# Where TensorE's rounded operands begin in SBUF: two blocks on one core

## What is computed

```python
def reference(x, ...):
    x = first_block(x, ...)      # one layer: four kinds of attention, gates, w_out, conv FFN (D_FF = 2816)
    return second_block(x, ...)  # two layers: FFN, four mixers, w_out, FFN, a gated embedding

def swiglu(x, w_gate, w_up, w_down):
    return (jax.nn.silu(x @ w_gate) * (x @ w_up)) @ w_down
```

## Time and profile before

| | |
|---|---|
| Median of 3 runs | 3416.65 us (3411.78 to 3417.28) |
| The profiled execution | 3416.89 us |
| Its span, first to last instruction | 3415.6 us |
| Mean granted clock of TensorE | 0.973 |
| Matmuls | 14,843 |
| Weights and inputs read | 268.6 MB, 79 GB/s over the span |
| Busy: PE, POOL, DVE, ACT | 95%, 65%, 43%, 22% |

### The profile page before, as it was taken

One profiled execution on the slowest core, in us unless ns is written; L12 is line 12 of the kernel. 1 busy time (PEld: TensorE's weight loads), 2 busy tenths in 40 slices (PEclk: granted clock), 3 DMA queues, 4 the chain that ended last, 5 costly groups with the idle time before them and its releaser, 6 DMA issues.

```text
span 3415.6 us, 38646 instructions
## 1 busy us (share of the span) xinstructions
PE 3249.3 (95%) x14843; PEld 2579.7 (76%) x14843; DVE 1478.6 (43%) x2242; ACT 741.5 (22%) x1335; POOL 2236.2 (65%) x2554
## 2 busy tenths in 40 slices
PE   7989999899999999989999999999999889999998
PEld 4766667688887888777677888778887767788886
DVE  2226542467715731267553231443314765533214
ACT  3223333222211110123231110211102333211103
POOL 3334545789978877753347777887777433577776
PEclk9999999999999999999999999999999989999999
DMA  4211112233333332321113333233333211233332
GB/s 130 52 50 47 50 53 74 68 93 99 94 98 95 99 99 93 94 67 39 41 56 93 94 95 101 81 99 96 96 99 89 54 42 39 68 94 98 93 103 76
DMA packets 469295, 273.22 MB, mean 80 GB/s; under 512 B 20926, under 2 KB 466288, under 8 KB 469112
## 3 DMA queue, kind: packets, MB, share of 16 engines
q1 hardware_dynamic: 468056, 268.65, 26.7%
q10 hardware_dynamic: 1056, 2.12, 0.2%
HBM read 268.58 MB, written 2.12 MB: 79 GB/s over the span
## 4 chain that ended last, share of the span: by engine, by line
PE 81%; DVE 4%; POOL 3%; ACT 1%; issue 1%; DVEq 0%; POOLq 0%; ACTq 0%
PE bank L654 16%; PE bank L655 15%; PE bank L659 15%; PE bank L1025 6%; PE bank L1019 6%; PE bank L1020 6%; DVE arena L1926 2%; POOL wl L619 2%; PE bank L1178 1%; PE bank L840 1%; PE bank L749 1%; PE bank L686 1%; PE bank L750 1%; PE bank L687 1%; PE bank L688 1%; PE bank L755 1%
## 5 line engine op out<-in xcount | busy, mean ns | idle before, releaser
L619 POOL TENSOR_TENSOR wl<-raw,wh 128x256 fp32r<-128x256 f32 x2040 | 1674.8, 852 | 42.5
L614 POOL TENSOR_SCALAR wh<-raw 128x1024 fp32r<-128x1024 f32 x510 | 563.8, 1105 | 1114.2 <-PE bank L659 436.4
L654 PE MATMUL bank<-xh,wh 128*128 128x512 f32 x1568 | 626.9, 400 | 3.3 <-ACT arena L1530 3.3
L655 PE MATMUL bank<-xl,wh 128*128 128x512 f32 x1568 | 617.9, 394 | 0.0
L1926 DVE TENSOR_TENSOR arena<-arena 128x512 f32<-128x512 f32 (+2 forms) x474 | 405.5, 873 | 104.4 <-ACT arena L1763 43.3
L659 PE MATMUL bank<-xh,wl 128*128 128x512 f32 x1568 | 390.1, 389 | 0.0
L1926 DVE TENSOR_TENSOR arena<-bank,nrm 128x512 f32<-128x512 f32 x236 | 152.0, 686 | 532.7 <-PE bank L659 532.5
L654 PEld LDWEIGHTS bank<-xh,wh 128*128 128x128 f32 x1568 | 299.6, 191 | 74.2 <-ACT arena L1530 3.4
L655 PEld LDWEIGHTS bank<-xl,wh 128*128 128x128 f32 x1568 | 299.3, 191 | 64.2 <-issue 2.2
L659 PEld LDWEIGHTS bank<-xh,wl 128*128 128x128 f32 x1568 | 294.4, 188 | 61.1
L654 PE MATMUL bank<-arena_rounded,wh 128*128 128x512 f32 x816 | 323.4, 396 | 0.0
(11 more groups left out here) (314 smaller groups left out, 4461.6 us busy)
## 6 DMA issues: line engine op xcount, KB each, us to landing
raw<-in_ffn_w_gate SPq DMA_DIRECT2D x176, 256.0 KB, 3.2
raw<-in_ffn_w_up SPq DMA_DIRECT2D x176, 256.0 KB, 3.2
raw<-in_ffn_w_down SPq DMA_DIRECT2D x176, 256.0 KB, 3.0
raw<-in_w_in SPq DMA_DIRECT2D x158, 256.0 KB, 3.3
raw<-in_w_up SPq DMA_DIRECT2D x88, 256.0 KB, 3.3
raw<-in_w_gate SPq DMA_DIRECT2D x64, 256.0 KB, 3.2
raw<-in_w_out SPq DMA_DIRECT2D x48, 256.0 KB, 3.1
raw<-in_w_down SPq DMA_DIRECT2D x44, 256.0 KB, 3.0
```

The costliest lines, as they stand in the source:

```text
L614: pool.tensor_scalar(wh[:, s, :], raw[:, s, :], 1.0, 0.0, ALU.mult, ALU.add).then_inc(split, 1)
L619: ins = pool.tensor_tensor(wl[:, s, c], raw[:, s, c], wh[:, s, c].bitcast(F32), ALU.subtract)
L654: pe.matmul(psum, cols(wh, i), xhi, start=(i == 0), stop=False)
L655: pe.matmul(psum, cols(wh, i), xlo, start=False, stop=False)
```

## The change

The calls that allocate buffers are put in another order, with two assertions and one buffer `between` of 48 numbers that nothing reads. Sizes, types, contents and every instruction stay as they are.

```diff
-    arena_at = (nc.sbuf_base + 31) // 32 * 32
-    arena = sb("arena", [P, ARENA])
-
-
-    ar = nc.alloc_sbuf_tensor_at("arena_rounded", [P, OPERANDS], F32R, offset=arena_at)
-
-    h = sb("h", [P, DC, S])
-
-    xh, xl = sb("xh", [P, DC, S], F32R), sb("xl", [P, DC, S], F32R)
-    op_hi, op_lo = sb("op_hi", [P, 4, S], F32R), sb("op_lo", [P, 4, S], F32R)
-
-    raw = sb("raw", [P, 2, PIECE])
-    wh, wl = sb("wh", [P, 2, PIECE], F32R), sb("wl", [P, 2, PIECE], F32R)
-    const = sb("const", [P, CONST_N])
     levels = sb("levels", [P, UNIT_LEVELS * P], U8)
     pcol = sb("pcol", [P, A_NROWS // 4 * 4])
     convw = sb("convw", [P, 3, 2 * FC])
-    lcol = sb("lcol", [P, LAYERS * L_NROWS])
     lbs = sb("lbs", [P, LAYERS, 4, NH])
     foxb = sb("foxb", [P, 1])
+
+
+    arena_at = (nc.sbuf_base + 31) // 32 * 32
+    assert arena_at % 256 == 0, arena_at % 256
+    arena = sb("arena", [P, ARENA])
+
+
+    ar = nc.alloc_sbuf_tensor_at("arena_rounded", [P, OPERANDS], F32R, offset=arena_at)
+
+    h = sb("h", [P, DC, S])
     rcol = sb("rcol", [P, TT])
     gains2 = sb("gains2", [P, DC])
+    stat = sb("stat", [P, 2, 4])
+    assert nc.sbuf_base % 256 == 0, nc.sbuf_base % 256
+
+    xh, xl = sb("xh", [P, DC, S], F32R), sb("xl", [P, DC, S], F32R)
+    op_hi, op_lo = sb("op_hi", [P, 4, S], F32R), sb("op_lo", [P, 4, S], F32R)
+
+    raw = sb("raw", [P, 2, PIECE])
+    eps = sb("eps", [P, 1])
+    const = sb("const", [P, CONST_N])
+    sb("between", [P, 48])
+    assert nc.sbuf_base % 256 == 0, nc.sbuf_base % 256
+    wh, wl = sb("wh", [P, 2, PIECE], F32R), sb("wl", [P, 2, PIECE], F32R)
+    lcol = sb("lcol", [P, LAYERS * L_NROWS])
     ones = sb("ones", [P, 3, P])
     nrm = sb("nrm", [P, 3, S])
-    stat = sb("stat", [P, 2, 4])
-    eps = sb("eps", [P, 1])
```

More of the change, by code:

```diff
@@ L220, in sem @@
         return ctx.enter_context(nc.semaphore(name))
+    levels = sb("levels", [P, UNIT_LEVELS * P], U8)
+    pcol = sb("pcol", [P, A_NROWS // 4 * 4])
+    convw = sb("convw", [P, 3, 2 * FC])
+    lbs = sb("lbs", [P, LAYERS, 4, NH])
+    foxb = sb("foxb", [P, 1])
     arena_at = (nc.sbuf_base + 31) // 32 * 32
+    assert arena_at % 256 == 0, arena_at % 256
     arena = sb("arena", [P, ARENA])
@@ L228, in program @@
     h = sb("h", [P, DC, S])
+    rcol = sb("rcol", [P, TT])
+    gains2 = sb("gains2", [P, DC])
+    stat = sb("stat", [P, 2, 4])
+    assert nc.sbuf_base % 256 == 0, nc.sbuf_base % 256
     xh, xl = sb("xh", [P, DC, S], F32R), sb("xl", [P, DC, S], F32R)
@@ L233, in program @@
     raw = sb("raw", [P, 2, PIECE])
+    eps = sb("eps", [P, 1])
+    const = sb("const", [P, CONST_N])
+    sb("between", [P, 48])
+    assert nc.sbuf_base % 256 == 0, nc.sbuf_base % 256
     wh, wl = sb("wh", [P, 2, PIECE], F32R), sb("wl", [P, 2, PIECE], F32R)
-    const = sb("const", [P, CONST_N])
-    levels = sb("levels", [P, UNIT_LEVELS * P], U8)
-    pcol = sb("pcol", [P, A_NROWS // 4 * 4])
-    convw = sb("convw", [P, 3, 2 * FC])
     lcol = sb("lcol", [P, LAYERS * L_NROWS])
[L240 to L243, removed]
     ones = sb("ones", [P, 3, P])
     nrm = sb("nrm", [P, 3, S])
-    stat = sb("stat", [P, 2, 4])
-    eps = sb("eps", [P, 1])
     def C(name, rows=slice(0, P)):
```

## The result

| | before | changed |
|---|---|---|
| median (lowest to highest), us | 3416.74 (4 runs) | 3384.56 (3381.33 to 3390.19, 4 runs) |
| ratio, 95% interval | | 0.9911 [0.9893, 0.9929] |
| profiled execution, span, us | 3416.89, 3415.6 | 3387.4, 3386.1 |

The changed kernel takes 32 us less by the medians and 29.5 us less by the two profiled spans. The forecast was 3387.

What follows compares the result with a forecast made beforehand. TensorE, busy 95% of the span, was taken as the bound, through the start-to-start distance of its matmuls. Terms of -29.0 and -1.0 us, the others 0, took 3416.9 to 3387 us; own range 3380 to 3395, full range 3376 to 3442.

Steps and rivals of the forecast that it cites:

- Item 1: 4464 matmuls streaming the arena: distance falls from 233.3 to 226.7 ns, 29.8 us, less 0.8 for waits: -29.0 us.
- Item 2: 8004 other rounded products: one place before and after, 0; settling in down-projections goes, 480 x 2 ns, -1.0 us.
- Item 3: Products of unrounded operands (scores, transposes, recurrence): place costs at most 1 ns there, so 0.
- Item 4: POOL's split of weights: arena stages lose 0.16 us per piece, which POOL's wait of 1.2 us covers.
- Item 5: VectorE, ScalarE, GpSimd and DMAs see other addresses: taken as 0, with 3 us either way kept for the range.
- The period rival: Period longer than 256: arena products gain 29.8 us, 7,020 others lose 46.8; 3434 or 3440 us, chance 0.13.
- The own-place rival: Only the streamed buffer's own place counts, 0 being like 128: all run at 233.3 ns, +46.8, 3463 us, chance 0.04.
- No change: Something other than place within 256 sets the arena products' distance: 3416.9 us stays, chance 0.08.
- Much faster: Place 0 is best and the whole loss over 213.3 ns per matmul goes: 183 us, 3234 us, chance 0.12.

Runs made afterwards that it cites:

- The raw kernels: Changed kernel with raw moved 4 or 8 bytes below a multiple of 256, eps and const behind wl: 3363.48 and 3365.95 us; with raw at 0, 3389.41 us.
- its control: Same buffers and addresses as the kernel with raw 4 bytes below, but raw beginning at 0 within 256 like wh and wl: 3389.41 us, ratio to before 0.9921.

## Why the prediction held, by its steps

**Item 1, the arena's products, -29.0: right.** The mechanism (5.60 to 5.44 us in g0) and the count (4464) came as worked out. By the count all is 29.8 us; the eight stages lost 28.0, item 2's part included. What is missing lies where PE waits at times: w_out gave 0.7 of 1.3 us, the down-projections with the gated embedding 1.9 and 2.4 of 2.9. So taking something off was right, and 0.8 was too little by some 1.5 us.

**Item 2, the 8004 others and their settling, 0 and -1.0: right in direction.** c stayed at 5.44, and `op_hi` in L1025 fell from 391 to 389 ns as said. In each of the down-projections of c, f0 and f1 the loss is 3.06 us, where 432 arena products x 6.67 ns are 2.88. The 0.18 over agree with the settling's share of 96 products x 2 ns.

**Item 3, unrounded products, 0: right.** 303 and 304 ns against 305 and 304.

**Item 4, POOL's slack: right.** The working took 0.16 of 1.2 us per piece; 0.95 was left, somewhat less than the 1.04 of the working.

**Item 5, the other engines, 0 within 3 us: right for this change, wrong as a reading.** I kept 3 us since no row told one place from another. The raw kernels show that a shift of raw of 4 bytes alone is worth 26 us against its control. The change moved raw and `wh` from 32 to 0 together, and POOL's subtraction stayed at 851 ns (852 before). The stages without arena products sum to 1.5 us less, out of moves of up to 4.8 us either way, so the term can't be told from 0. The 25 ns more of VectorE's operation may be in the 4.8 us that layer 1's mixers took longer; no run parts that.

**Luck in the number.** The forecast of 3387, the profiled 3387.4 and the median of 3384.56 agree better than the working earns: the four runs spread from 3381.33 to 3390.19, and the eight stages' 28.0 us, 2 short of the working's 30.0, met 1.5 us in stages where no arena product stands. What the prediction had right is the step per product.

**The period rival** (0.13) put c at 5.6 us after. It is at 5.44 with xh 243 x 256 bytes from wh, and the odd multiple of 256 alone gives 226.8 ns: out. **The own-place rival** (0.04) is out for 0, 32 and 96, but off multiples of 32 the place does count besides the distance (both at 4: 237.8 ns), a case that neither kernel has. **No change** (0.08) is out. It followed the Trainium skill, "SBUF — State Buffer", section "Who interferes with whom", by which TensorE's two read ports are independent and it waits on no one; here the same product alone on the chip takes 226.7 to 240.0 ns by the places of its operands, so for two operands of TensorE itself the measurement goes against it. **Much faster** (0.12) needed a place with little or no loss: of 36 distances at 512 columns and seven common places none was below 226.66 ns. The 215.7 ns of the Trainium skill, "TensorE: Matmul & The Clock Gate", section "Wait — 56ns, not 53.3ns?", was seen in no run here.

**One aside was wrong**: that the 32 cycles left at one place read like the price of a weight load sharing the memory. With a quarter of the weight columns the load itself falls from 188 to 109 ns, and the matmul takes 231.7 ns and not less; with half of them 230.0, with 96 of 128 230.1 and with 112 228.9. What the 32 cycles are is still open, and so is why distances such as 64, 104 and 248 lie between 226.7 and 233.3.

## What to carry to other kernels

Where TensorE is the bound and streams 512 columns of rounded float32, start both operands of a product at one place within 256 bytes and at a multiple of 32 (for 256 columns another distance was better), and read the effect from the start-to-start distance in the chain, not from mean durations. Work it out per buffer from the order of allocation before touching anything else, since one small buffer ahead decides it for all behind it. Try the same for the inputs of GpSimd's subtractions, where here the first input a few bytes lower was the better place.

## What the runs showed of the hardware that was not expected

- The cost by distance isn't smooth, nor the same in both directions: 4 apart 236.7 ns, 252 apart 226.7, 60 apart 226.7, 68 apart 236.7, 120 apart 240.0, all with the weights at 0. With the streamed operand at 0 and the weights moved, the kernel gave 232.4 ns for 252 and 233.3 for 4.
- A streamed operand at the place of the next product's weights took 230.0 ns, at that of its own 233.9, and at both 226.7.
- GpSimd's subtraction of two SBUF inputs took 851 ns with both inputs at one place within 256 and 751 to 753 with the first 4 or 8 bytes lower, but 850 with it 4 bytes higher (the kernel with the weights 4 below) and 848 to 850 with it 160, 128 or 192 bytes away (those with the weights at 96, 128 and 64). VectorE's subtraction or addition sped up beside it, 1080 to 988 ns. That GpSimd's instruction holds something that VectorE needs for a shorter time would explain this; no run parts that from other causes, and none shows what makes 4 and 8 lower the good places.
